# Dense gates: the slot's weight moves from the compared row factor into the second pass over the column factor

## The reference, cut to what matters

```python
s = jnp.einsum('thpk,hpnk->thpn', q, sub_keys)          # 8 heads, 2 x 128 keys
s1, i1 = lax.top_k(s[:, :, 0], 16); s2, i2 = lax.top_k(s[:, :, 1], 16)
cand = (s1[..., :, None] + s2[..., None, :]).reshape(T, 8, 256)
cand_idx = (i1[..., :, None] * 128 + i2[..., None, :]).reshape(T, 8, 256)
top_s, pos = lax.top_k(cand, 16)
idx = jnp.take_along_axis(cand_idx, pos, axis=-1)
g = jax.nn.softmax(top_s, axis=-1)                       # 128 slots a token
out = sum over the slots of g * gelu(expert_u[idx] . h) * expert_v[idx]
```

## Time and profile before

| | us |
|---|---|
| three runs | 1919.1, 1919.5, 1921.91 |
| median | 1919.5 |
| the profiled execution | 1916.59 |
| its span | 1914.8 |

### The profile page before, as it was taken

How to read it: one execution, slowest core, us unless ns; L and a number is a source line. 1 busy time by engine, 2 the same in 40 slices (tenths; PEclk the granted TensorE clock), 3 DMA queues, 4 the chain that set the end, 5 groups by cost and what they waited for, 6 DMA issues and landing times.

```text
span 1914.8 us, 29466 instructions
## 1 busy us (share of the span) xinstructions
PE 1762.5 (92%) x9782; PEld 1456.5 (76%) x9782; DVE 1497.3 (78%) x3051; ACT 663.5 (35%) x1103; POOL 796.7 (42%) x646
## 2 busy tenths in 40 slices
PE   5799998797899999379999999999999999999994
PEld 2444446546788888369999999999999999999993
DVE  1311017534999999979999999999999999999997
ACT  1110015501177665123333333333333333333332
POOL 1400000000000000258887887778766666666661
PEclk9999998999999999689999999999999999999997
DMA  9921110240025445689999999999999999999993
GB/s 358 386 74 50 44 44 1 110 176 34 1 59 119 89 89 112 206 342 396 398 406 404 391 400 407 407 402 404 394 407 407 406 402 400 397 401 407 407 402 142
DMA packets 253537, 520.88 MB, mean 272 GB/s; under 512 B 113953, under 2 KB 130977, under 8 KB 252193
## 3 DMA queue, kind: packets, MB, share of 16 engines
q1 hardware_dynamic: 178016, 249.00, 36.5%
q0 software_dynamic: 73728, 268.47, 35.4%
q10 hardware_dynamic: 1730, 2.59, 0.4%
HBM read 488.54 MB, written 31.46 MB: 272 GB/s over the span
## 4 chain that ended last, share of the span: by engine, by line
PE 53%; DVE 24%; issue 13%; DMA 5%; ACT 3%; DVEq 1%; SPq 0%; POOL 0%; ACTq 0%; POOLq 0%
DVE arena L1112 11%; PE ps L1474 9%; PE ps L1473 9%; PE ps L1472 9%; PE ps L1229 7%; PE ps L1392 5%; PE ps L1373 4%; PE ps L1443 3%; DMA arena_w<-in_w_mod 3%; DMA U_in<-in_expert_uT 2%; DVE V_lo L1074 2%; PE ps L1271 1%; DVE C_lo L1087 1%; PE ps L1198 1%; PE ps L1429 1%
## 5 line engine op out<-in xcount | busy, mean ns | idle before, releaser
L1472 PE MATMUL ps<-hT_hi,U_hi 128*128 128x384 f32 x1024 | 344.3, 336 | 29.6 <-DVE U_lo L1069 29.6
L1474 PE MATMUL ps<-hT_hi,U_lo 128*128 128x384 f32 x1024 | 344.5, 336 | 0.0
L1473 PE MATMUL ps<-hT_lo,U_hi 128*128 128x384 f32 x1024 | 343.7, 336 | 0.0
L1472 PE MATMUL ps<-V_hi,C_hi 128*128 128x512 f32 x768 | 300.8, 392 | 12.0 <-DVE C_lo L1087 12.0
L1474 PE MATMUL ps<-V_hi,C_lo 128*128 128x512 f32 x768 | 302.9, 394 | 0.0
L1473 PE MATMUL ps<-V_lo,C_hi 128*128 128x512 f32 x768 | 302.7, 394 | 0.0
L1472 PEld LDWEIGHTS ps<-hT_hi,U_hi 128*128 128x128 f32 x1024 | 192.9, 188 | 34.6 <-issue 29.7
L450 POOL DMA_INDIRECT arena<-in_expert_u,idxn x128 | 176.9, 1382 | 100.1 <-DVE arena L1101 38.8
L707 ACT CAST V_hi<-V_in 128x1024 fp32r<-128x1024 f32 x128 | 135.0, 1055 | 236.4 <-PE ps L1474 236.4
L715 ACT ACTIVATE act_t<-ps 128x384 f32<-128x384 f32 x128 | 63.0, 492 | 410.1 <-PE ps L1474 410.1
L450 POOL DMA_INDIRECT arena<-in_expert_v,idxn x128 | 159.5, 1246 | 93.3 <-DVE arena L1112 41.3
(11 more groups left out here) (223 smaller groups left out, 3096.4 us busy)
## 6 DMA issues: line engine op xcount, KB each, us to landing
U_in<-in_expert_uT SPq DMA_DIRECT2D x128, 512.0 KB, 9.0
V_in<-in_expert_v SPq DMA_DIRECT2D x128, 512.0 KB, 6.2
arena_w<-in_w_mod SPq DMA_DIRECT2D x12, 2048.0 KB, 12.6
gates_scratch<-arena_w SPq DMA_DIRECT2D x6, 4096.0 KB, 21.0
gate_in<-gates_scratch SPq DMA_DIRECT2D x128, 192.0 KB, 7.2
arena_w<-in_w_in SPq DMA_DIRECT2D x4, 2048.0 KB, 12.4
arena_w<-in_w_query SPq DMA_DIRECT2D x1, 7168.0 KB, 21.3
arena_w<-in_w_out SPq DMA_DIRECT2D x2, 2048.0 KB, 7.7
```

The source lines that it names most:

```text
L1472: nc.tensor.matmul(out, hi, rhi, start=start, stop=False)
L1473: nc.tensor.matmul(out, hi, rlo, start=False, stop=False)
L1474: return nc.tensor.matmul(out, lo, rhi, start=False, stop=stop)
```

## The change

In `one_hot` the second pass becomes four instructions, one for each token of the quad, Relu(weight - 4 x square) with the weight as the bias: the weight (at most 1) where the key matches, else 0, since the least other square is 1. In `sel_out` a wait for the copy of `selT` stands ahead of the one-hots. In `gate_rows` the four compares with weight become one compare of all four tokens, without the weight, with both operands broadcast.

```diff
 act.wait_ge(s_dsq, q + 1)
-act.activation(lhs1[q % LR], lhs1[q % LR], ACT.Relu, bias=1.0, scale=-1.0).then_inc(s_lhs1, 1)
+b, at = q // QUADS + 1, q % QUADS * QUAD
+for t in range(QUAD):
+    ins = act.activation(lhs1[q % LR][:, t, :], lhs1[q % LR][:, t, :], ACT.Relu,
+                         bias=selT[:, b % 2, 1, at + t:at + t + 1], scale=-4.0)
+ins.then_inc(s_lhs1, 1)
...
 act.copy(selT[:, b % 2], ps[:, 6, 0:2 * P].rearrange("p (w t) -> p w t", w=2)).then_inc(s_selT, 1)
+act.wait_ge(s_selT, b)
 for p in range(LR - 1):
     one_hot((b - 1) * QUADS + p)
...
-for t in range(QUAD):
-    at = p * QUAD + t
-    ins = dve.tensor_scalar(rhs1[q % RR1][:, t, :], iota[:, :], selT[:, b % 2, 0, at:at + 1],
-                            selT[:, b % 2, 1, at:at + 1], ALU.is_equal, ALU.mult)
-ins.then_inc(s_rhs1, 1)
+rows_of = selT[:, b % 2, 0, p * QUAD:(p + 1) * QUAD]
+dve.tensor_tensor(rhs1[q % RR1], iota[:, :].unsqueeze(1).broadcast_to([P, QUAD, NKEY]),
+                  rows_of.unsqueeze(2).broadcast_to([P, QUAD, NKEY]), ALU.is_equal).then_inc(s_rhs1, 1)
```

## The result

| | before | changed |
|---|---|---|
| median, 5 runs each, us | 1919.35 | 1929.23 |
| the profiled execution | 1916.59 | 1929.23 |
| its span | 1914.8 | 1927.4 |

The ratio is 1.0055, 95% interval 1.0043 to 1.0067: 10.6 us slower on 1919.35 (8.3 to 12.9). Forecast was +7.3.

What follows compares the result with a forecast made beforehand. TensorE was taken as the bound, waiting on ScalarE's `query_out` and VectorE's row factors. +3.16 us a block, +9.5 over three, less 2.2 in the last ranking: +7.3 us, median 1926.8, range 1917 to 1934.

Steps and rivals of the forecast that it cites:

- The bound and its place: TensorE's scores (L1402) wait 0.65 us for ScalarE's `query_out`, behind the second pass; to become about 1.7, once a block 3.
- The price of a piece: ScalarE's second pass: each pointer-bias piece about 390 ns, one every 0.29 us, so +0.63 us a quad.
- rival 1: Pointer cost hidden on ScalarE, pieces every 0.20 us: -3.6 us in all, 1915.9; chance 0.19, shared with another rival.
- p=8: +2.40: First score of a dense block, behind three one-hots and quads 0 to 6 on ScalarE: 2.40 us later.
- p=16: +1.02: Second score of a dense block: 20.53 us after the first score instead of 19.51, so 1.02 us more.
- rival 2: ScalarE dearer, pieces every 0.31 us, or TensorE's clock falls after a longer idle: +13.7 us, 1933.2; chance 0.19.
- p=24: +0.86: Third score of a dense block: 20.53 us after the second instead of 19.75, plus 0.08 refill: 0.86 us more.
- p=24 to 32: -1.12: End of a dense block: TensorE's waits for VectorE's row factors go, 1.12 us less; the last wait of 0.36 stays.
- The last ranking: -2.2: Fifth ranking, after the blocks: VectorE's lead gains 2.2 us before group 3 needs TensorE's score.
- Costed at nothing: The new wait on `s_selT` in `sel_out`, before the one-hots: predicted to cost nothing.

Runs made afterwards that it cites:

- after_early: The changed kernel with ScalarE's `query_out` issued one quad earlier; ratio 0.9941 to the kernel before, second block 77.1 us.
- four_const: The kernel before with the second pass cut into four pieces of 128x128, constant bias 1.0, no pointer; ratio 1.0009, stage (first `selT_fill` to `hT_lo`) +1.7 us.
- v_alone: The kernel before with only VectorE's one unweighted compare a quad, ScalarE's second pass as before; ratio 0.9969, stage (first `selT_fill` to `hT_lo`) -5.8 us.
- after_filled: The changed kernel with TensorE's four matmuls of quad 7 in each block issued four times instead of once; ratio 1.0033 to the kernel before, stage +7.4 us.
- s_alone: The kernel before with only ScalarE's four pointer-bias pieces and the wait on `s_selT`, VectorE's weighted compares kept; ratio 1.0063, stage +14.9 us.

## Why the prediction was right

- **The bound and its place.** Right. The waits of L1402 for `query_out` became 2.98, 1.63 and 1.69 (I had said about 3 and about 1.7), and after_early shows that it was the order that made them dear.
- **The price of a piece.** 0.386 us and one every 0.30, against 0.39 and 0.29. The extrapolation from L584 and L605 held, and rival 1, the hidden pointer, fell: four_const is what its ScalarE side would have looked like, +1.7, and with v_alone's -5.8 that is about -4 (an estimate from two runs) where the rival had -3.6.
- **p=8: +2.40.** Measured 22.01 less 19.63, **+2.38**.
- **p=16: +1.02.** This term was mis-sized: 22.11 less 19.51 is **+2.60**. The 1.6 too many are the score and the query behind it at half clock. The idle before it was forecast, but not what it does to the clock. I had that only as a second way to rival 2 ("makes TensorE's granted clock fall for some microseconds") and not in the sum; after_filled gives 1.6 us a block for it, 4.8 in three, and that is what the sum lacked: with the gap filled this step is 20.49, +0.98, and the stage +7.4, against the 1.02 and 7.3 forecast. The trace of before could have warned me: there too the clock stood at 0.50 behind an idle, one of 4.46 us at the start of the first block (last section). I had looked only at the second block, with idles of 0.8 at most.
- **p=24: +0.86, p=24 to 32: -1.12.** The 19.75 of the prediction came from the chain of the earlier trace rows, which counts this score only from the end of the group before it (660.40). The timeline, which gives all the other scores, has it at 660.23:

```profile
660.23 1.05 PE L1402 MATMUL ps<-arena 128*128 128x128 f32 x8
```

So before it was 19.58 and 19.06, and measured are 20.55, **+0.97**, and 17.93, **-1.13**. Both right within 0.11 us, and v_alone shows the uncovered wait that ties them.

- **The last ranking: -2.2.** 41.2 less 43.4, right; s_alone, without VectorE's lead, does not have it. The later spill of the gates cost nothing that shows.
- **Costed at nothing:** the wait on `s_selT`, +0.2 in the stage, within what two profiles differ.
- **The sum.** 9.5 - 2.2 = 7.3 forecast, 12.2 in the stage of the profiled run (14.4 for three blocks, less 2.2), 10.6 by the ratio. The last two agree within the interval (8.3 to 12.9); the forecast is just outside it. Direction, path and the other terms were right, and the range held because it took in rival 2. Of that rival the price, c = 0.31, did not come true, and its second way, the clock, did: with 13.7 it is as near to the measured time as the forecast is, and in the stage nearer.

## What to carry to other kernels

An engine that is a third idle can still be the one that others wait for: before giving it more work, find what stands behind this work in its order, and who waits for that. A copy that another engine waits for belongs ahead of a long step that nobody wants yet; one line of order was worth twice here what the change cost. And a small idle that grows may cost more than its length, once the idle engine's clock falls.

Here the order also set the sign: with the copy behind the long step the change cost 12.2 us in the stage, with the copy ahead of it the change gained 5.1.

## What I had not expected of the hardware

TensorE's granted clock fell to 0.50 after an idle of 2.98 us in the midst of a stretch in which it was otherwise busy all the time, and stayed there until about 3.5 us after work resumed (629.43 to about 633); after 1.63 and 1.69 us, in the same block, it did not fall. In the first block it fell with an idle of 2.75 us (the score behind it took 2.05), and in s_alone with one of 2.73 (2.05). Where between 1.69 and 2.73 us it begins, or whether the length of the idle alone decides, no run here shows.

The kernel before has one such place, at the start of its first block, by the timeline of TensorE and by stretch:

```profile
518.81 0.48 PE L1417 MATMUL ps<-ident,sel 128*128 128x128 f32 x1 [4.46 <-DVE gates L1025]
...
520.00:521.00 1.00, 1.00 (x3) 0.39 (x4) 1.00 (x9) 0.00 (x0) 0.00 (x0) 0.50 0.00 0
```
